# Last tile's out-projection item by item, three weight loads held behind a gather, and rotary tables made after the first norms

## What is computed

```python
def hybrid_layer(x, pos, g_pre, w_in, ...):          # block 1, two layers
    h = rmsnorm(x, g_pre) @ w_in                     # first thing that TensorE has to do
    ...
    q = concat(q_nope, rope(q_rope, pos))            # cos and sin tables of the positions
    ...
    return x + rmsnorm(y @ w_out, g_post)

for l in range(DEPTH):                               # block 2, two layers
    proj = h @ w_in[l]
    ...
    mix = concat(o_dn, o_sa) @ w_out[l]              # the out-projection
    h = layer_norm(ALPHA * h + mix, ln1_g[l], ln1_b[l])
    ffn = hier_moe(h, ...)      # group by top-1, two experts in the group, rows gathered
    h = layer_norm(ALPHA * h + ffn, ln2_g[l], ln2_b[l])
```

## Time and profile before

| | |
|---|---|
| median of 3 runs | 1377.95 us (1377.4 to 1380.56) |
| the profiled execution's own time | 1376.68 us |
| its span in the trace | 1374.9 us, so 1.8 us lie around it |
| granted TensorE clock, mean | 0.985 of full |
| TensorE busy | 1308.2 us (95% of the span) |
| TensorE's share of the chain of work that ended last | 77% |
| VectorE busy, ScalarE busy | 573.2 us (42%), 486.8 us (35%) |
| moved by DMA | 307.18 MB, 223 GB/s over the span |

### The profile page before, as it was taken

The page is one execution under the profiler, slowest core; times in us unless marked ns, Lnnn a source line. Parts: engine busy times, 40 slices in busy tenths (PEclk is TensorE's granted clock), DMA queues, the critical chain, the costliest instruction groups (busy, mean ns, idle before and its releaser), DMA issues.

```text
span 1374.9 us, 18995 instructions
## 1 busy us (share of the span) xinstructions
PE 1308.2 (95%) x7405; PEld 837.5 (61%) x7405; DVE 573.2 (42%) x1246; ACT 486.8 (35%) x1065; POOL 44.5 (3%) x63
## 2 busy tenths in 40 slices
PE   6999989999999999998999999899999989999996
PEld 5778567785688877654443443688887644443432
DVE  2334312343468485353222223668485341231224
ACT  4245432453464234421222232564234412223232
POOL 0000000000002000000000000002000000000000
PEclk9999999999999999998999999999999999999999
DMA  9553252232422132647999999322133766999994
GB/s 364 115 150 102 82 212 98 92 104 80 185 96 94 38 117 99 266 191 278 404 421 422 421 421 415 118 96 94 37 118 118 281 251 265 419 420 423 421 420 188
DMA packets 48846, 307.18 MB, mean 223 GB/s; under 512 B 5897, under 2 KB 6409, under 8 KB 16752
## 3 DMA queue, kind: packets, MB, share of 16 engines
q1 hardware_dynamic: 43760, 288.61, 52.9%
q0 software_dynamic: 3200, 8.16, 2.7%
q10 hardware_dynamic: 1792, 9.12, 1.8%
HBM read 300.86 MB, written 8.59 MB: 225 GB/s over the span
## 4 chain that ended last, share of the span: by engine, by line
PE 77%; DVE 13%; ACT 6%; DMA 3%; issue 2%; ACTq 0%; DVEq 0%; POOLq 0%
PE ps L1075 22%; PE ps L1739 17%; PE ps L1766 8%; PE ps L1326 4%; PE ps L1115 4%; PE ps L1808 2%; PE ps L1829 2%; DMA normed_rows<-res 1%; DMA arena<-normed_rows,group_tokens 1%; PE ps L1548 1%; DVE projT L2659 1%; DVE small L2658 1%; PE ps L1748 1%; PE ps L1538 1%; PE ps L1790 1%
## 5 line engine op out<-in xcount | busy, mean ns | idle before, releaser
L1075 PE MATMUL ps<-hT,ring 128*128 128x272 f32 (+1 forms) x1984 | 473.9, 393 | 4.6 <-ACT hT L1940 1.7
L1075 PEld LDWEIGHTS ps<-hT,ring 128*128 128x128 f32 x1984 | 373.5, 192 | 78.7 <-issue 9.3
L1739 PE MATMUL ps<-ring,arena 128*64 128x512 f32 x416 | 138.5, 598 | 0.0
L3012 DVE TENSOR_TENSOR xo<-ps,xo 128x512 fp32r<-128x512 f32 x64 | 42.9, 689 | 99.4 <-ACT xo L2344 99.4
L1739 PE MATMUL ps<-projT,arena 128*64 128x512 f32 x240 | 80.0, 597 | 0.0
L3003 DVE TENSOR_TENSOR arena<-arena,ps 128x256 f32<-128x256 f32 x32 | 13.5, 422 | 139.9 <-ACT arena L2331 139.4
L1739 PEld LDWEIGHTS ps<-ring,arena 128*64 128x64 f32 x416 | 40.0, 137 | 52.0 <-issue 51.2
L2071 ACT ACTIVATE projT<-ps 128x272 f32<-128x272 f32 x68 | 27.0, 397 | 116.6 <-PE ps L1075 115.0
L2329 ACT ACTIVATE arena<-ps 128x256 f32<-128x256 f32 x32 | 12.3, 383 | 137.8 <-PE ps L1739 137.8
L1326 PE MATMUL ps<-ring,projT 128*128 128x512 f32 x128 | 56.6, 596 | 0.0
L1115 PE MATMUL ps<-ring,arena 128*128 128x512 f32 x128 | 55.9, 593 | 0.0
(11 more groups left out here) (502 smaller groups left out, 2005.1 us busy)
## 6 DMA issues: line engine op xcount, KB each, us to landing
ring<-experts SPq DMA_DIRECT2D x72, 1024.0 KB, 17.2
ring<-w_in SPq DMA_DIRECT2D x62, 1024.0 KB, 4.8
projT<-experts SPq DMA_DIRECT2D x48, 1024.0 KB, 16.1
arena<-experts SPq DMA_DIRECT2D x22, 1024.0 KB, 12.2
prm<-experts SPq DMA_DIRECT2D x22, 1024.0 KB, 17.1
ring<-w_out SPq DMA_DIRECT2D x16, 1024.0 KB, 4.9
spare<-experts SPq DMA_DIRECT2D x12, 1024.0 KB, 14.9
lent<-experts SPq DMA_DIRECT2D x8, 1024.0 KB, 10.7
```

The lines of the kernel that those rows point to most:

```text
L1075: mm = pe.matmul(ps[:, 5 + j % banks, 0:ncols], w[:, j % 2, k, :], hT[:, k, T - ncols:T], start=(k == 0), stop=(k == KC - 1))
L1739: mm = pe.matmul(ps[64 * e:64 * e + 64, 0, :], xg[:, 4 * h + k, i % 2, 64 * e:64 * e + 64], w[e][:, k // 2, 512 * (k % 2):512 * (k % 2) + ...
L3012: v.tensor_tensor(low, ps[:, 4 + half, :], high, ALU.subtract).then_inc(s("pair_rows_copied"), 1)
```

## The change

Five edits. (1) SyncE loads `x` before the constants. (2) VectorE squares and sums tile 2 of `x` itself, while ScalarE does tile 1; the eleven operations of the rotary tables come after the scaling, the first three of them between the four even copies of the transposed rows, and TensorE starts on tile 1's scaled rows as soon as these and the constants are there. (3) Tile 2's out-projection takes both halves of an item together, in the order of the items, and TensorE frees each of the first three items as it is done with it. (4) The transposes of tile 1 for the router stand after the second item of tile 2, its logits after the third. (5) Items 14 to 16 of the experts also wait for `rows_fetched`, the first group's gathered rows.

```diff
-            sp.dma_start(cst[:, 0:head], A["consts"][:, 0:head]).then_inc(start_in, 16)
             for t in (1, 2):
                 sp.dma_start(res[:, t, :], A["x"][0, (t - 1) * P:t * P, :]).then_inc(x_in[t - 1], 16)
+            sp.dma_start(cst[:, 0:head], A["consts"][:, 0:head]).then_inc(start_in, 16)
...
                     if j == 7 + MORE_SLOTS + ITEMS_WO:
                         sp.wait_ge(layer_normed, normed_at[l, 1, 2, 1])
+                        sp.wait_ge(rows_fetched, 16 * (GROUPS * l + 1))
...
-            pe.wait_ge(tables_vec, 18)
+            pe.wait_ge(tables_vec, 7)
+            pe.wait_ge(start_in, 32)
...
+                    if k == 0 and t:
+                        pe.wait_ge(tables_vec, 8)
...
-                    for half in range(2 if t == 2 else 1):
-                        for i, pair in enumerate(OUT_ORDER):
...
-                                    for h in (half,) if t == 2 else (0, 1):
...
-                            if half and i == 0:
-                                router_turn(0, 1)
-                            if half and i == 1:
-                                router_logits(0, 1)
-                        mm.then_inc(s("out_projected"), 1)
+                    for i, pair in enumerate(OUT_ORDER):
...
+                                for h in range(2):
+                                    mm = pe.matmul(ps[:, (4 if t == 1 else 2) + h, :], rows(pair, c),
+                                                   weights(i)[:, c, 512 * h:512 * h + 512], start=first, stop=last)
+                                    if t == 2 and last:
+                                        mm.then_inc(s("out_projected"), 1)
+                        if t == 2 and not last:
+                            mm.then_inc(ring_used, 1)
+                        if t == 2 and i == 1:
+                            router_turn(0, 1)
+                        if t == 2 and i == 2:
+                            router_logits(0, 1)
+                    if t < 2:
                         mm.then_inc(s("out_projected"), 1)
...
-            a.wait_ge(tables_vec, 18)
             for k in range(1, KC, 2):
...
-            a.wait_ge(tables_vec, 16)
+            a.wait_ge(tables_vec, 19)
             L0(a.activation(sinT, sinT, ACT.Sin))
...
-                            a.sem_inc(ring_used, ITEMS_WO)
+                            a.sem_inc(ring_used, 1)
...
+            v.wait_ge(x_in[1], 16)
+            V0(v.scalar_tensor_tensor(out=yT[:, 4:8, :].rearrange("p a n -> p (a n)"), in0=res[:, 2, :], scalar=1.0,
+                                      in1=res[:, 2, :], op0=ALU.mult, op1=ALU.mult, accum_out=ssum[:, 2:3]))
+            for t in (1, 2):
+                v.wait_ge(tables_done, 3 if t == 1 else 5)
+                if t == 1:
+                    v.wait_ge(x_in[0], 16)
+                V0(v.tensor_scalar(xn[:, t - 1, :], res[:, t, :], rstd[:, t:t + 1], None, ALU.mult))
```

More of the change, by code:

```diff
@@ L1310, in rows @@
                         return mix_chunk(2 * pair + c)[:, COL[t]:COL[t] + ROWS[t]]
-                    for half in range(2 if t == 2 else 1):
-                        for i, pair in enumerate(OUT_ORDER):
-                            if t == LN_ORDER[0]:
-                                item_in(pe, (2, l, ITEMS_P2 + i))
-                                pe.wait_ge(s("delta_gated") if pair < 2 else s("mixed_copied"), 2 * (pair % 2) + 2)
-                            for c in range(2):
-                                first, last = i == 0 and c == 0, i == ITEMS_WO - 1 and c == 1
-                                if t == 0:
-                                    for q in range(4):
-                                        mm = pe.matmul(ps[32 * q:32 * q + META, 0, 0:256], rows(pair, c),
-                                                       weights(i)[:, c, 256 * q:256 * q + 256], start=first, stop=last)
-                                else:
-                                    for h in (half,) if t == 2 else (0, 1):
-                                        mm = pe.matmul(ps[:, (4 if t == 1 else 2) + h, :], rows(pair, c),
-                                                       weights(i)[:, c, 512 * h:512 * h + 512], start=first, stop=last)
-                            if half and i == 0:
-                                router_turn(0, 1)
-                            if half and i == 1:
-                                router_logits(0, 1)
@@ new lines, in mix_out @@
+                    for i, pair in enumerate(OUT_ORDER):
+                        if t == LN_ORDER[0]:
+                            item_in(pe, (2, l, ITEMS_P2 + i))
+                            pe.wait_ge(s("delta_gated") if pair < 2 else s("mixed_copied"), 2 * (pair % 2) + 2)
+                        for c in range(2):
+                            first, last = i == 0 and c == 0, i == ITEMS_WO - 1 and c == 1
+                            if t == 0:
+                                for q in range(4):
+                                    mm = pe.matmul(ps[32 * q:32 * q + META, 0, 0:256], rows(pair, c),
+                                                   weights(i)[:, c, 256 * q:256 * q + 256], start=first, stop=last)
+                            else:
+                                for h in range(2):
[9 more added lines that the diff above has]
+                            router_logits(0, 1)
@@ L1905, in _ @@
             for t in (1, 2):
-                a.wait_ge(x_in[t - 1], 16)
-                L0(a.activation(yT[:, 0:4, :], res[:, t, :], ACT.Square, accum_out=ssum[:, t:t + 1]))
+                if t == 1:
+                    a.wait_ge(x_in[0], 16)
+                    L0(a.activation(yT[:, 0:4, :], res[:, 1, :], ACT.Square, accum_out=ssum[:, 1:2]))
+                else:
+                    a.wait_ge(tables_vec, 6)
                 rsqrt_act(a, L0, rstd[:, t:t + 1], ssum[:, t:t + 1], 1.0 / D, eps6, None)
@@ L2419, in _ @@
                 if l == 0:
-                    for k in range(0, KC, 2):
-                        v.wait_ge(head_turned, k + 1)
-                        VT(v.tensor_scalar(hT[:, k, META:T], ps[:, k % 4, 0:SEQ], prm1("g_pre")[:, k:k + 1], None, ALU.mult),
-                           head_vec)
+                    rotary_tables()
                 strict4 = bc(const("strict"), 4, 1)
@@ L2443, in _ @@
                         v.wait_ge(s("latent_rotated"), 1)
-                        v.wait_ge(tables_done, 8)
+                        v.wait_ge(tables_done, 7)
                         v.wait_ge(late_in, 16)
```

35 lines of the change are left out of this document (21 added, 14 removed).

## The result

| | before | changed |
|---|---|---|
| median | 1377.4 us (1374.2 to 1380.56, 5 runs) | 1364.1 us (1363.53 to 1368.14, 5 runs) |
| profiled execution | 1376.68 us, span 1374.9 | 1368.14 us, span 1366.3 |
| mean granted clock | 0.985 | 0.987 |

The ratio is 0.9913, with a 95% interval of 0.9888 to 0.9938: faster by 0.9%. The profiled execution of the changed kernel is the slowest of its five, so its trace shows less of a lead (8.6 us of span) than the medians (13.3 us).

A forecast was written before the change was run, and what follows sets the result against it. TensorE, busy in 95% of the span, was taken as the bound, so only its waits count: 1.3 + 4.0 + 6.3 = 11.6 us off 1376.68 makes 1365.1, or 1366.4 for a median; range 1361.8 to 1372.

The forecast's parts named there:

- start: Program start: transposes begin 1.6 us before 12.77, less 0.3 of stall in the projection, so 1.3 us won.
- layer 0's gather: Wait for layer 0's gathered rows: gather_pair starts at 624.2 instead of 628.19, 4.0 us won.
- layer 1's gather and clock: Wait for layer 1's gathered rows: gather_pair 4.8 us earlier, experts 1.5 sooner by full clock; 6.3 us in all.
- The stall at chunk 2: First projection: TensorE waits 0.3 us ahead of chunk 2, as ScalarE's copy comes later behind the moved tables.
- Out-projection at no cost: Tile 2's out-projection: VectorE's second half starts at 605.25 as before; cost 0, at most 0.1 us a layer.
- The held items: Ahead of both gathers: store alone takes 2.6 us instead of 9.14 and 8.68, gather 4.2; 4.0 and 6.3 us won.
- The stream follows: Experts' weights: the stream resumes as much earlier as TensorE, at 631.4 and 1137.1, so the gain is kept.
- (a): Both gathers: the gather is slow by itself, 6.8 us, giving 1370 us; chance 0.12.
- (b): Entry to the grouped experts: TensorE comes 2.7 us late out of the branch in both layers, 1372 us; chance 0.08.
- (d): End of each layer: the time goes to the weights' stream and TensorE waits there, 1376.5 us; chance 0.06.
- (e): SyncE's queue hangs on a gather beyond 8.6 us (10.7 in layer 1); at 12 us slower, 1381.3 us; chance 0.04.
- (c): More gain: x lands early, clock recovers within layer 0's gather, each worth 1 to 2 us, 1363 us; chance 0.14.

The follow-up runs named there:

- c_again: The changed kernel itself, run once more without any edit: median 1365.11 us, ratio 0.9915 against the kernel before.
- b_warm: Changed kernel plus twelve matmuls of zeros ahead of the first transposes: 1364.37 us, ratio 0.9919 against before.
- s_out: Kernel before with only tile 2's out-projection item by item, its slots freed one by one: 1366.78 us, ratio 0.9927.
- s_hold: Kernel before with only the added wait of items 14 to 16 for the fetched rows: 1364.89 us, ratio 0.9925.
- s_mid: Kernel before with both middle edits (out-projection item by item, held items), start as before: 1365.74 us, ratio 0.9925.
- c_tables: Kernel before with VectorE's sum of squares and the late tables, but constants still loaded ahead of x: 1377.45 us, ratio 1.0002.
- b_stored: Changed kernel with the three weight items waiting for the stored rows instead of the fetched rows: 1364.42 us, ratio 0.9913 against before.
- b_trim: Changed kernel with other keep_busy sizes, more filling in layer 0 and less in layer 1's last: 1363.67 us, ratio 0.9904 against before.

## Why the prediction was right

The forecast was 1366.4 us with 1364 to 1369 for the likeliest case; 1364.1 and 1365.11 were measured. For the profile, whose sum counts, `c_again` is the fairer partner, since it has no extra stretches of half clock in layer 1's mixer (480.0 us from layer 0's first expert matmul to layer 1's last out-projection block in the changed profile, 477.3 in `c_again`, 477.1 before), and its time of 1364.88 lies near the medians. Its span of 1363.1 is 11.8 below before's; the sum was 11.6. The two gathers, 10.3 us of it, came out as predicted, mechanism and size. That the whole fits to 0.2 us is luck: the start brought 1.0 less than I said, and 1.4 came from a stretch for which I had put nothing. By its terms:

| term | predicted | measured |
|---|---|---|
| start | 1.3 | 0.3 (in four profiles; 1.5 to 1.8 in four) |
| first block and layer 0's mixer | 0 | 1.4 |
| layer 0's gather | 4.0 | 3.9 |
| layer 0's experts, layer 1's mixer | 0 | -0.3 |
| layer 1's gather and clock | 6.3 | 6.6 |
| to the end | 0 | -0.1 |

**Start.** *"That is 1.6 us before 12.77."* It is 2.05, as `x` landed sooner: ScalarE's square began at 6.58 and VectorE's took 1.23 us, not 1.4. The stall at chunk 2 was predicted as 0.3 us and is 0.36 and 0.38 where TensorE was at full pace (0.72 in `b_warm`, which started the projection sooner). What failed is the step "Start: 1.6 - 0.3 = 1.3 us": I took TensorE's pace in the projection as given. It was not: 64 records took 14.08 us before and 16.02 now, and this is most of what became of the 2.26 us. By layer 0's out-projection the lead is 1.75 us (1.71 in `c_again`) all the same, but this can't be put down to the edits: `s_out` and `s_hold`, which have before's code up to there, reach it at 598.28 and 598.38, before at 601.62. So 3.3 us of scatter lie in that stretch, and the clock accounts for it. Added up from the granted clock in windows of 20 us up to 600, TensorE was at half clock for about 17.6 us in before, 14.4 in the changed kernel and in `c_again`, and 10.4 in `s_out` and `s_hold`. As an estimate, a us at half clock costs half a us: 3.6 us between before and `s_out`, and 1.6 of the 1.75 that the changed kernel seemed to have won. A part of it may go with the start: in the window of 160 to 200 us the granted clock is 0.96 in five of the six profiles with late full pace (`s_mid` among them), and 0.91 in the sixth, `c_tables`, and in the eight others.

**Out-projection at no cost.** Right: VectorE's second half starts at 603.50, 1.75 before 605.25, exactly the lead that TensorE had. But I also gave it no share in the gain, and by itself it wins 3.9 and 5.4 us. I had seen the reason, *"Three `w_out` slots come free 5 to 13 us earlier"*, and not drawn the conclusion that this alone empties the queues ahead of the gather.

**The held items.** *"the store is alone: 2.6 us"*: measured 2.6 in both layers. The gather was taken at 4.2, and measured at 3.3 and 4.2; it starts 0.8 to 0.9 behind `group_tokens`. The price of layer 0 came out at 3.87 for 4.0, since not `keep_busy` but `psel` stands last there, at nearly the same moment. Layer 1 behaved to the letter: `gather_pair` directly behind `keep_busy`, at full clock, 1.78 for 3.41 us. What the runs add is that a short store is not what pays: with 8.0 us of it `s_hold` gained as much in layer 0.

**The stream follows.** Right. Item 17 was issued 5.5 us sooner, 1.75 of it the lead that TensorE had already. TensorE waits 1.3 and 0.3 us for weights at the end of the changed profile for 1.1 before, and from layer 1's first expert matmul to the end the changed kernel takes 235.8 us and before 235.2; `c_again` takes 235.3.

**The rivals.** (a) falls with 3.3 and 4.2 us for the gather; `b_stored` shows that its 5.8 to 6.8 needs weights beside it, and there it costs 1.7 us in all, not the 3.6 that (a) says, as `psel` and the filling cover it. (b) falls: `gather_pair` waits 0.17 us in layer 0 and none in layer 1, while at the other end of layer 0's experts the wait is 2.81 for 2.71. What the Trainium skill ("Runtime: NRT & Kernel Launch", Instruction fetch mechanics) states is narrower than I put it there: the fetch is forced where the target of the taken branch lies outside the instructions held, and no trace here shows whether it does. (d) and (e) needed a gather beyond 8.6 us; (e) called 8.22 the nearest, but under full traffic before's gathers reach 9.2. Of (c), `x` did land early, but with TensorE's slow pace it was worth little; the clock did not recover within layer 0's gather.

## What to carry to other kernels

A transfer on which an engine waits was slow here by the bytes issued ahead of it, and landed with the last of them: add up what is issued before it and is not yet through, at the measured rate, and see whether its issue falls behind that. Leave room, since the last item landed 2.8 to 6.1 us behind such a sum (`b_stored`, `s_hold`, before). If two bursts together reach over it, moving either away may be enough, and the two edits' gains do not add; run each alone before you keep both. And a gain at the start of a program counts only once the next two limits are known, here the pace of TensorE's first matmuls and a copy on ScalarE behind two table loads. Before a lead in one profile is put down to an edit, compare the granted clock of the stretch.

## What the runs showed of the hardware

- At the start of the program the row of the granted clock reads 1.00, while TensorE works at half pace until 19 to 21 us in six of 14 profiles; in the eight others the first projection, which starts at 14.3 to 18.4 us, runs at full pace throughout. It differs between executions of the same start. Records of 128x256 take up to 795 ns for 379 (`c_again`), and the count of records in a window shows it (5 in 2 us for 11).
- A gather of 128 rows (512 KB) with nothing beside it takes 3.3 us in layer 0 and 4.2 in layer 1 (changed), and 3.3 to 3.4 and 4.2 to 4.3 in the seven other kernels with an edit of the middle and no such burst; with 3 MB of weights released 5.4 and 4.3 us ahead of it, 5.8 and 6.8 (`b_stored`); behind seven items 6.8 and 8.2 (before). It lands with the last of the weights ahead of it, within 0.8 us.
- In `b_trim` the granted clock fell to 0.50 near 619.1 us in layer 0 although TensorE had been busy for 1.66 us of the two from 616 and stood still for at most 0.39 us at a time; in layer 1, with similar filling, it stayed at 1.00.
- Stretches at half clock in TensorE's busy mixers differ between executions of the same code: about 10.4 us up to 600 us in `s_out`, 17.6 in before.
